# Part of a recurrence moved beside another stage's product, and attention tiles in alternating order

## The chip, the cores and the metric

One core of a Trainium2 chip runs the whole program once. The metric is the device time of one execution in microseconds, taken as the median of several runs. A profile of one further execution shows every instruction of TensorE (PE), its weight loads (PEld), VectorE (DVE), ScalarE (ACT), GpSimd (POOL) and the DMA queues.

## What is computed

Two blocks follow one another on 1024 tokens of width 1024, in fp32. The change touches the second block, after its input projection:

```python
q, k, v, xr, gr = jnp.split(proj, [...], axis=-1)       # 4 heads x 2 x 64 of q and k, 512 v, 512 xr, 512 gr
q = partial_rope(rms_norm_2(q, q_norm_w[l]), cos, sin)
k = partial_rope(rms_norm_2(k, k_norm_w[l]), cos, sin)
lam = exp(sum(lambda_q1 * lambda_k1)) - exp(sum(lambda_q2 * lambda_k2)) + lambda_init
attn = diff_attention(q, k, v, lam)                     # (softmax_0 - lam * softmax_1) @ v, causal, tiles of 128 queries
attn = rms_norm_2(attn, subln_w[l]) * (1.0 - lambda_init)
xc = causal_dwconv(xr, conv_rnn_w[l], conv_rnn_b[l])    # 4 taps
y = rg_lru(xc, w_gate_a[l], b_gate_a[l], w_gate_x[l], b_gate_x[l], lru_lambda[l])
y = rms_norm_2(y * jax.nn.gelu(gr), rnn_norm_w[l])
x = x + jnp.concatenate([attn, y], axis=-1) @ w_out[l]
```

In rg_lru two gates r and i are sigmoids of block-diagonal products of xc; a = exp(-8 r softplus(-lambda)), u = sqrt(1 - a^2) i xc, and h[t] = a[t] h[t-1] + u[t] along the 1024 tokens.

## The kernel before

Stages follow one another, each a block in which every engine has its own in-order list of instructions and waits on semaphores. The order of work is written out by hand. Names and lines are those of the program in the profile.

**mix** (line 2195) merges the first block's branches, projects them with w_out, normalizes, and multiplies by the second block's input weights. Products of fp32 accuracy are made of three matmuls on split operands (product3). After 128 tiles of merging come j = 0 to 31, tiles of 128 channels x 512 tokens: 16 for q and k, 8 for xr, 8 for gr. VectorE evicts each one with a per-token factor (L2555); turn_head (L2481 to L2488) normalizes and rotates q and k; ScalarE makes the head norms with Ln and Exp and then gelu of gr (L2361). Then come j = 32 to 47, the v product: 16 tiles of 128 tokens x 256 channels in two column halves c, evicted by ScalarE (L2368). Six PSUM buffers rotate; two more banks (6 and 7) are for sums.

**attend** (line 2582) makes attention and the recurrence together. Its 32 units n are (head h, query tile t), t from 0 to 7, of width (t+1)*128 keys. For unit n:
- TensorE: sc(n), the scores of both softmaxes into one set of four PSUM banks (L2656), with the mask added (L2659); then tr(n-1), the transposes (L2667); then av(n-2), the product with v (L2678). sc(n) waits for both exponentials of n-1.
- VectorE: soft(n-1), the combination of the two softmaxes (L2883 to L2890), then peak(n, 0) and peak(n, 1), the maxima (L2876).
- ScalarE: exp(n, 0) and exp(n, 1) with their sums (L2738), turn_out(n-1), the copy of the transposes (L2746), take(n-2), the copy of the output (L2753).

The setup of small vectors stands before unit 0 (L2845 to L2867). After a head: square, mean, norm, scale, flip (L2699) and end (L2771, L2772). One channel group of the recurrence goes with each head: tap (convolution, L2914, L2917), gates (L2693, 128 x 128 weights, two halves of 512 tokens), open_a, open_x, decay, decay2, bend, rise on ScalarE (L2778 to L2806), and admit, spare, enter, run, leave on VectorE (L2922 to L2943; run is the scan over tokens, L2937). Each is hung on a fixed tile t of the head. The stage ends with the last head's end; then **out_up** (line 2980) begins, with the output projection.

The ring of two weight buffers feeds each product in split form: ring.load on SyncE waits until the buffer's low part is cut (ring.cut), split_hi on ScalarE (L138) and split_lo on VectorE (L145) make the two parts.

## Time and profile before

| | us |
|---|---|
| median of 3 runs | 4651.68 (4647.18 to 4652.19) |
| the profiled execution's own time | 4653.29 |
| its span | 4651.5 |
| TensorE busy | 4501.1 (97%) |
| VectorE busy | 2670.2 (57%) |
| ScalarE busy | 1727.7 (37%) |
| mean granted clock of TensorE | 0.985 |

A page has busy time by engine, the span in slices, queues, a chain and groups of instructions. The stage of attention lies between 3547.7 and 3748.7 us of the span, the v product of mix just before it. A timeline shows instructions in order of their start, with equal neighbours merged, and in brackets how long the engine had stood idle and what released it. The granted clock is 1.00 at 2.4 GHz and 0.50 at 1.2 GHz.

### The profile page before, as it was taken

To read this page: it belongs to the slowest core of one execution; us is meant where nothing else is said; L and a number is where in the kernel's file an instruction comes from. 1 tells how busy PE (TensorE), PEld (TensorE's weight loads), DVE (VectorE), ACT (ScalarE), POOL (GpSimd) and SP (SyncE) were. 2 spreads that over 40 slices of the span, in tenths; PEclk is the share of its full clock that TensorE was granted. 3 is DMA by queue.
4 is the path that set the end of the run, shared out by engine and by line. 5 is a ranking of instruction groups with operands and counts; after the bars stand their busy time and mean duration, and the time that the engine had idled before them with its cause. 6 is when DMAs were issued, how large, how long until landed. Compare 5 with 4: busy or idle time off the path is not lost. (4 is left out here: it accounts for less than half of the span.)

```text
span 4651.5 us, 66517 instructions
## 1 busy us (share of the span) xinstructions
PE 4501.1 (97%) x27608; PEld 3667.2 (79%) x27608; DVE 2670.2 (57%) x3938; ACT 1727.7 (37%) x2924; POOL 457.6 (10%) x371
## 2 busy tenths in 40 slices
PE   7999999999999999999999799899998789999999
PEld 4888877778999999999999444688776567888887
DVE  3245545555637777777777676546453755555543
ACT  3234443444424544455444333211343742111111
POOL 0000000000002333332336000000010000000000
PEclk9999999999999999999999999999999899999999
DMA  5244344434430110111021352433210021122222
GB/s 210 99 144 151 130 147 141 145 131 150 168 120 15 46 57 30 64 41 59 28 102 45 98 178 86 155 108 109 82 46 19 19 113 63 70 77 73 100 87 95
DMA packets 155978, 441.79 MB, mean 95 GB/s; under 512 B 17168, under 2 KB 47120, under 8 KB 140448
## 3 DMA queue, kind: packets, MB, share of 16 engines
q1 hardware_dynamic: 140624, 383.98, 23.5%
q0 software_dynamic: 9296, 32.58, 2.0%
q10 hardware_dynamic: 5760, 20.97, 1.2%
q8 instruction: 221, 3.62, 0.3%
q14 instruction: 77, 0.63, 0.0%
HBM read 294.86 MB, written 141.56 MB: 94 GB/s over the span
## 5 line engine op out<-in xcount | busy, mean ns | idle before, releaser
L202 PE MATMUL pr_ps<-uhl,w_split 128*128 128x512 f32 (+1 forms) x1520 | 586.7, 386 | 3.1 <-DVE w_split L145 2.2
L206 PE MATMUL pr_ps<-uhl,w_split 128*128 128x512 f32 (+1 forms) x1520 | 571.9, 376 | 0.0
L205 PE MATMUL pr_ps<-uhl,w_split 128*128 128x512 f32 (+1 forms) x1520 | 571.2, 376 | 0.0
L1583 DVE TENSOR_TENSOR b_G<-b_ps,cst 128x512 fp32r<-128x512 f32 x560 | 381.5, 686 | 65.0 <-PE b_ps L1362 61.7
L138 ACT ACTIVATE w_split<-share 128x2048 fp32r<-128x2048 f32 x64 | 122.6, 1915 | 701.1 <-DVE ou_vc L3305 271.1
L202 PEld LDWEIGHTS pr_ps<-uhl,w_split 128*128 128x128 f32 x1520 | 287.0, 189 | 81.4 <-issue 29.2
L205 PEld LDWEIGHTS pr_ps<-uhl,w_split 128*128 128x128 f32 x1520 | 287.1, 189 | 56.0 <-issue 5.8
L206 PEld LDWEIGHTS pr_ps<-uhl,w_split 128*128 128x128 f32 x1520 | 286.8, 189 | 52.3
L1124 POOL TENSOR_SCALAR b_Mr<-b_tri 128x512 fp32r<-128x512 f32 x80 | 117.8, 1489 | 1878.9 <-DVE b_tri L1567 1878.9
L202 PE MATMUL ou_ps<-ou_a,w_split 128*128 128x512 f32 x704 | 277.5, 394 | 7.7 <-DVE ou_a L2160 7.7
L205 PE MATMUL ou_ps<-ou_a,w_split 128*128 128x512 f32 x704 | 275.6, 391 | 0.0
L206 PE MATMUL ou_ps<-ou_a,w_split 128*128 128x512 f32 x704 | 275.3, 391 | 0.0
L776 DVE COPY pr_stage<-pr_ps 128x256 f32<-128x256 f32 (+1 forms) x92 | 49.7, 540 | 391.7 <-PE pr_ps L206 391.6
L202 PE MATMUL mx_ps<-mx_a,w_split 128*128 128x512 f32 x640 | 258.1, 403 | 13.4 <-DVE mx_a L2160 13.4
L1214 ACT ACTIVATE b_EY<-b_ps 128x512 fp32r<-128x512 f32 x320 | 192.4, 601 | 183.1 <-PE b_ps L1376 183.1
L206 PE MATMUL mx_ps<-mx_a,w_split 128*128 128x512 f32 x640 | 255.3, 399 | 0.0
L205 PE MATMUL mx_ps<-mx_a,w_split 128*128 128x512 f32 x640 | 254.0, 397 | 0.0
L1362 PE MATMUL b_ps<-b_G,b_EY 128*128 128x128 f32 x1600 | 244.8, 275 | 0.0
L1362 PEld LDWEIGHTS b_ps<-b_G,b_EY 128*128 128x128 f32 x1600 | 222.4, 190 | 12.6 <-issue 12.0
L206 PE MATMUL ou_ps<-ou_ext,w_split 128*128 128x512 f32 x576 | 224.4, 390 | 0.0
L202 PE MATMUL ou_ps<-ou_ext,w_split 128*128 128x512 f32 x576 | 224.3, 389 | 0.0
L205 PE MATMUL ou_ps<-ou_ext,w_split 128*128 128x512 f32 x576 | 224.3, 389 | 0.0
(498 smaller groups left out, 10045.5 us busy)
## 6 DMA issues: line engine op xcount, KB each, us to landing
w_ring<-in_w_in SPq DMA_DIRECT2D x41, 1024.0 KB, 5.3
proj<-pr_stage SPq DMA_DIRECT2D x160, 256.0 KB, 2.0
share<-in_w_up SPq DMA_DIRECT2D x24, 1024.0 KB, 4.8
ar<-share SPq DMA_DIRECT2D x32, 512.0 KB, 2.8
b_AR<-ar SPq DMA_DIRECT2D x64, 256.0 KB, 2.9
pr_raw<-proj SPq DMA_DIRECT2D x48, 256.5 KB, 3.4
ada<-in_ada_w SPq DMA_DIRECT2D x24, 512.0 KB, 5.8
ff<-ou_vc ACTq DMA_DIRECT2D x24, 512.0 KB, 2.6
```

The source lines that it names most:

```text
L138: self.nc.scalar.activation(self.hl[:, n % NBUF, 0], raw, ACT.Copy).then_inc(self.hi_done, 1)
L202: mm = nc.tensor.matmul(dst, a[0], b[0], start=start, stop=False)
L205: nc.tensor.matmul(dst, a[0], b[1], start=False, stop=False)
L206: return nc.tensor.matmul(dst, a[1], b[0], start=False, stop=stop)
L776: V.tensor_copy(dst, src).then_inc(taken[1], 1)
L1124: F[x]["pool"].done(ts(Mr[x][:], tri[x][e][:], 1.0, None, ALU.mult), f"{n}.Mr")
L1214: L[x]["act"].done(A(EY[x][:, 0:2], both(x)[:, 0:2], ACT.Copy), f"{n}.low{m}")
L1362: mm = mmul(bank(x, 0)[:, q * P:(q + 1) * P], E[x][:, q] if m else Mr[x][:, q], Gs[x][m % 2][:, q], start=True, stop=True)
L1583: L[x]["dve"].done(V.tensor_tensor(Gs[x][m % 2][:], heads(x, 0 if m else 1), rep(K(f"lev{m}"), 4), ALU.mult), f"{n}.G{m}")
```

## The change

In mix, the small vectors of the recurrence and lambda are made between the evictions of the q/k product (lower at j = 4, rates at j = 20). The convolutions of all four channel groups run on VectorE from j = 28 on; the gates, the ScalarE passes and the scans of groups 0 and 1 run beside the v product, and their results are written over gr. Gates use PSUM banks 6 and 7. Buffers are taken from the weight ring's raw halves, from xr of the two done groups and from the rope table. In attend, groups 2 and 3 are left, their convolutions (in the former table) already there; their steps are hung on chosen units from n = 1 to 9 and 12 to 25. Odd heads take their tiles from 7 down to 0. The norm of a head's output is done in five groups (three whole heads, then two halves of head 3), one half of each head's last copy goes to VectorE, and the sums of exponentials are kept, so that a copy per unit goes. Table sets of ScalarE are loaded at written places. TensorE gets small products of ones after units 17 and 18 and before the last flip. Cut to the lines that the text speaks of (scale, mean, square, norm and end take a group g instead of a head; they and the recurrence's steps are otherwise as before):

```diff
+        few = small(rn)
+        lp, lam, sub_w, hb, l0, l1 = (few[n] for n in ("lp", "lam", "sub_w", "hb", "l0", "l1"))
+        early_w, late_w = ([ring.buf[:, (ring.base + 2 * RP + l) % NBUF].rearrange("p k c -> p (k c)")[:, f * T:(f + 1) * T] for f in range(2)] for l in (8, 9))
+        xc = [table[:, 0], table[:, 1]]
+        wg = early_w[1].rearrange("p (a k c) -> p a k c", a=2, k=RT)
...
                     ring.load(sp, w2[n] if n < 8 else w_v2[n - 8], 0, 0, 2 * RP + n, split=True)
+                sp.wait_ge(ring.cut, ring.split_base + 2 * RP + 11)
+                sp.dma_start(wg[:, 0], w_ga).then_inc(wg_in, 16)
...
+                nc.scalar.preload_act_table_set("natural_log_exp_and_others")
...
+                nc.scalar.preload_act_table_set("exp_and_others")
...
+                def rise(k):
+                    nc.scalar.preload_act_table_set("sqrt_and_others")
+                    act.wait_ge(m_ready, k + 1)
+                    A(tt[k], tt[k], ACT.Sqrt, scale=0.25).then_inc(rt, 1)
+                    nc.scalar.preload_act_table_set("exp_and_others")
...
+                    if j == 33:
+                        open_a(0)
+                    if j == 35:
+                        open_x(0)
+                        bend(0)
+                        decay(0)
+                        decay2(0)
+                    if j == 37:
+                        open_a(1)
+                        rise(0)
+                    if j == 39:
+                        open_x(1)
+                        bend(1)
+                    if j == 40:
+                        decay(1)
+                        decay2(1)
+                    if j == 41:
+                        rise(1)
                 act.wait_ge(bent, 8)
...
+                def gates(k, x):
+                    if x:
+                        pe.wait_ge(th_a, k + 1)
+                    else:
+                        pe.wait_ge(conv, k + 1)
+                        if k:
+                            pe.wait_ge(th_x, k)
+                        else:
+                            pe.wait_ge(wg_in, 32)
+                            pe.wait_ge(h_log, KT)
+                    for half in range(2):
+                        mm = nc.tensor.matmul(ps[:, 6 + half], wg[:, x, k], xc[k][:, half * HALF:(half + 1) * HALF], start=True, stop=True)
+                    mm.then_inc(gate_x if x else gate_a, 1)
                 for c in range(2):
...
+                        if c == 0 and t % 2 == 0:
+                            gates(t // 4, t // 2 % 2)
...
+                    if j >= 28:
+                        tap(0, j - 28)
                 ring.split_lo(dve, 2 * RP + 9)
+                for j in range(4):
+                    tap(1, j)
+                for k in range(2):
+                    admit(k)
+                    spare(k)
+                    enter(k)
+                    run(k)
+                    leave(k)
+                    for j in range(4):
+                        tap(k + 2, j)
                 dve.wait_ge(h_done, KT)
                 dve.wait_ge(taken, N1 + 32)
+                dve.wait_ge(conv, RT)
...
+    NR = 2
...
-        units = [(h, t) for h in range(A_HEADS) for t in range(T // P)]
+        units = [(h, 7 - t if h % 2 else t) for h in range(A_HEADS) for t in range(T // P)]
...
+        groups = [(0, 0, 8), (1, 0, 8), (2, 0, 8), (3, 4, 8), (3, 0, 4)]
+        rows_done = [8, 16, 24, 28, 32]
...
                 for k in range(RT):
-                    sp.wait_ge(y_ready, k + 1)
-                    sp.dma_start(cat[:, 4 + k], y[:, k % 2]).then_inc(y_stored[k % 2], 16)
-                for b in range(2):
-                    sp.wait_ge(y_stored[b], 8 * RT)
+                    if k >= RT - NR:
+                        sp.wait_ge(y_ready, k - (RT - NR) + 1)
+                    sp.dma_start(cat[:, 4 + k], gr[:, k]).then_inc(y_stored, 16)
+                sp.wait_ge(y_stored, 16 * RT)
...
+                def keep_warm(times):
+                    for _ in range(times):
+                        nc.tensor.matmul(ps[:, 1, 0:P], G["ones"][:], G["ones"][:], start=True, stop=True)
                 for n in range(NU):
-                    h, t = units[n]
                     sc(n)
-                    if t == 1:
-                        gates(h, 0)
-                    if t == 2:
-                        gates(h, 1)
-                    if t == 0 and h >= 2:
-                        pe.wait_ge(exp_ready, 2 * n)
-                        flip(h - 2)
+                    if n in (1, 12):
+                        gates(n // 12, 0)
+                    if n in (2, 13):
+                        gates(n // 12, 1)
+                    if n == 15:
+                        flip(0)
+                    if n == 28:
+                        flip(1)
+                    if n == 30:
+                        flip(2)
                     if n >= 1:
                         tr(n - 1)
                     if n >= 2:
                         av(n - 2)
+                    if n == 17:
+                        pe.wait_ge(head_out, 2)
+                    if n in (17, 18):
+                        keep_warm(4)
                 tr(NU - 1)
                 av(NU - 2)
-                pe.wait_ge(exp_ready, 2 * NU)
-                flip(A_HEADS - 2)
+                flip(3)
                 av(NU - 1)
-                flip(A_HEADS - 1)
+                pe.wait_ge(head_out, 6)
+                keep_warm(8)
+                flip(4)
 
...
+                    if n in (3, 14):
+                        bend(n // 12)
+                    if n in (4, 20):
+                        decay2(n // 20)
+                    if n in (5, 21):
+                        decay(n // 20)
+                    if n in (6, 22):
+                        nc.scalar.preload_act_table_set("sqrt_and_others")
+                        rise(n // 20)
+                        nc.scalar.preload_act_table_set("natural_log_exp_and_others")
+                    if n == 9:
+                        square(0)
+                    if n == 11:
+                        norm(0)
+                        nc.scalar.preload_act_table_set("exp_and_others")
+                    if n == 15:
+                        end(0, 0)
+                    if n == 17:
+                        square(1)
+                    if n == 23:
+                        norm(1)
+                    if n == 25:
+                        square(2)
+                    if n == 27:
+                        norm(2)
+                    if n == 28:
+                        end(1, 0)
+                    if n == 29:
+                        square(3)
+                    if n == 30:
+                        end(2, 0)
                 turn_out(NU - 1)
                 take(NU - 2)
+                norm(3)
                 take(NU - 1)
-                square(A_HEADS - 1)
-                end(A_HEADS - 2)
-                norm(A_HEADS - 1)
-                end(A_HEADS - 1)
+                square(4)
+                end(3, 1)
+                norm(4)
+                end(4, 0)
...
+                    if n in (3, 14):
+                        admit(n // 12)
+                    if n in (5, 21):
+                        spare(n // 20)
+                    if n in (7, 23):
+                        enter(n // 20)
+                    if n in (8, 24):
+                        run(n // 20)
+                    if n in (9, 25):
+                        leave(n // 20)
+                    if n == 10:
+                        mean(0)
+                    if n == 12:
+                        scale(0)
+                    if n == 15:
+                        end(0, 1)
+                    if n == 18:
+                        mean(1)
+                    if n == 26:
+                        scale(1)
+                    if n == 27:
+                        mean(2)
+                    if n == 28:
+                        end(1, 1)
+                    if n == 29:
+                        scale(2)
+                    if n == 30:
+                        mean(3)
+                        end(2, 1)
                 soft(NU - 1)
-                leave(RT - 1)
-                mean(A_HEADS - 1)
-                scale(A_HEADS - 1)
-                dve.wait_ge(y_ready, RT)
+                scale(3)
+                mean(4)
+                scale(4)
+                dve.wait_ge(y_ready, NR)
 
 
 FT = 24
@@ -3393,13 +3588,13 @@
```

## Rows read from the trace of the kernel before

**Rows 1.** The page's first line.
```profile
span 4651.5 us, 66517 instructions
```
**Rows 2.** Windows, one for each head: busy us (and instructions) by engine, granted clock, DMA.
```profile
core 0: us, PE busy (x) PEld busy (x) DVE busy (x) ACT busy (x) POOL busy (x), PEclk, DMA share, GB/s
...
3548.00:3592.00 44.00, 29.42 (x144) 17.20 (x144) 33.16 (x69) 29.29 (x60) 0.00 (x0) 0.84 0.11 36
3592.00:3637.00 45.00, 34.80 (x180) 24.27 (x180) 34.68 (x63) 31.70 (x65) 0.00 (x0) 0.85 0.03 13
3637.00:3684.00 47.00, 35.88 (x190) 24.68 (x190) 34.61 (x63) 32.89 (x66) 0.56 (x1) 0.85 0.06 23
3684.00:3730.00 46.00, 37.27 (x188) 26.03 (x188) 31.59 (x60) 32.73 (x66) 0.54 (x1) 0.81 0.06 24
```
**Rows 3.** Timeline, one widest tile: start, us, engine, line, operation, [idle before].
```profile
3631.11 1.99 PE L2656 MATMUL at_ps<-qk 64*128 64x512 f32 x8 [1.60 <-ACT at_p L2738]
...
3633.39 2.35 DVE L2876 TENSOR_REDUCE at_nb<-at_ps 128x1 f32<-128x1024 f32 x2
...
3634.65 1.11 ACT L2738 ACTIVATE at_p<-at_ps,at_nb 128x1024 f32<-128x1024 f32 x1 [2.73 <-DVE at_nb L2876]
...
3637.03 0.49 PE L2656 MATMUL at_ps<-qk 64*128 64x128 f32 x4 [1.29 <-ACT at_p L2738]
```
**Rows 4.** Timeline of TensorE, head 0: scores of tiles 0, 1, 5 and 6.
```profile
3548.33 0.49 PE L2656 MATMUL at_ps<-qk 64*128 64x128 f32 x4
...
3554.05 1.22 PE L2656 MATMUL at_ps<-qk 64*128 64x256 f32 x4 [4.86 <-ACT at_p L2738]
...
3573.09 1.56 PE L2656 MATMUL at_ps<-qk 64*128 64x512 f32 x8 [1.50 <-ACT at_p L2738]
...
3577.93 1.77 PE L2656 MATMUL at_ps<-qk 64*128 64x512 f32 x8 [1.11 <-ACT at_p L2738]
```
**Rows 5.** Timeline of TensorE, after the first tile of head 2.
```profile
3640.89 1.97 PE L2667 MATMUL at_ps<-cst,at_p 128*128 128x128 f32 x8 [2.09 <-DVE at_p L2890]
...
3645.77 0.83 PE L2656 MATMUL at_ps<-qk 64*128 64x256 f32 x4
```
**Rows 6.** Timeline of TensorE: a gate product and what follows it.
```profile
3602.12 1.93 PE L2693 MATMUL at_ps<-at_xc,at_wg 128*128 128x512 f32 x4
3603.89 0.27 PE L2667 MATMUL at_ps<-cst,at_p 128*128 128x128 f32 x1
```
**Rows 7.** Windows, the v product from its second tile on (columns as in rows 2).
```profile
3503.60:3546.80 43.20, 43.16 (x360) 42.95 (x358) 2.29 (x1) 8.92 (x17) 0.00 (x0) 1.00 0.00 1
```
**Rows 8.** Timeline of ScalarE: a table load and the activation after it.
```profile
3620.52 1.28 ACT L2765 ACT_TABLE_LOAD   x1
3621.82 0.21 ACT L2765 ACTIVATE at_fac<-at_fac 128x8 f32<-128x8 f32 x1
```
**Rows 9.** Groups by line, attention: busy us, mean ns | idle before.
```profile
L2917 DVE SCALAR_TENSOR_TENSOR at_xc<-xg,par,at_xc 128x1024 f32<-128x1024 f32 x12 | 15.3, 1275 | 0.1
...
L2937 DVE TENSOR_TENSOR_SCAN at_xc<-at_aa,at_ix 128x1024 f32<-128x1024 f32 x4 | 9.1, 2280 | 0.0
...
L2797 ACT ACTIVATE at_a<-at_ra,at_hb 128x1024 f32<-128x1024 f32 x4 | 5.1, 1287 | 0.0
...
L2922 DVE SCALAR_TENSOR_TENSOR at_ix<-at_ix,at_xc 128x1024 f32<-128x1024 f32 x4 | 4.9, 1216 | 0.0
```
**Rows 10.** Timeline, from the last exponential to the next stage.
```profile
3729.85 0.19 ACT L2738 ACTIVATION_READ_ACCUMULATOR at_p<-at_ps,at_nb 128x1 f32 x1
...
3738.11 0.28 ACT L2753 ACTIVATE at_raw<-at_ps 128x128 f32<-128x128 f32 x1 [2.38 <-PE at_ps L2678]
...
3741.48 1.28 ACT L2765 ACT_TABLE_LOAD   x1
...
3748.74 0.63 ACT L166 ACTIVATE w_split<-share 128x512 fp32r<-128x512 f32 x1 [0.97 <-PEq L2586]
```
**Rows 11.** Windows, the start of the next stage (columns as in rows 2).
```profile
3748.70:3756.00 7.30, 4.37 (x12) 3.47 (x13) 6.34 (x8) 6.06 (x8) 0.00 (x0) 0.55 0.91 359
```

More of the change, by code:

```diff
@@ L2489, in _, with run, leave @@
+                def run(k):
+                    dve.wait_ge(u_ready, 2 * k + 2)
+                    dve.wait_ge(ex, k + 1)
+                    V.tensor_tensor_scan(xc[k], aa[k], ix[k], 0.0, ALU.mult, ALU.add).then_inc(scan, 1)
+                def leave(k):
+                    dve.wait_ge(scan, k + 1)
+                    dve.wait_ge(bent, 8)
+                    V.tensor_tensor(gr[:, k], xc[k], gr[:, k], ALU.mult).then_inc(left, 1)
                 for k in range(HK):
@@ L2641, in _ @@
             def _(pe):
-                pe.wait_ge(lstep, 1)
-                nc.tensor.matmul(ps[:, 7, 0:2], K("heads64"), lp[:], start=True, stop=True).then_inc(lam_s, 1)
                 pe.wait_ge(rounded, 2)
@@ new lines, in end, with open_a @@
+                def end(g, x):
+                    h = groups[g][0]
+                    act.wait_ge(flipped, g + 1)
+                    if h >= 2:
+                        act.wait_ge(head_stored[h % 2], 16)
+                    A(out[:, h % 2, x * HALF:(x + 1) * HALF], flat_at(h, x), ACT.Copy, scale=sub_w).then_inc(head_out, 1)
+                def open_a(q):
+                    k = RT - NR + q
+                    act.wait_ge(gate_a, q + 1)
+                    if q:
+                        act.wait_ge(tn, q)
```

422 lines of the change are left out of this document (224 added, 198 removed).

## The prediction

> **What bounds the kernel now.** Read the page first: TensorE is busy nearly everywhere, and only one stretch of the 4651.5 us span stands out [rows 1]. The table of windows by head of attention shows it [rows 2]: from 3548 to 3730 TensorE is busy 29 to 37 us of each 44 to 47, at a mean granted clock of 0.81 to 0.85. No engine is full there; VectorE and ScalarE have 32 to 35 and 29 to 33. So the time of a head is a chain of hand-overs, and the next view is the timeline of one tile. A widest tile (1024 keys) runs from the start of its scores at 3631.11 to the start of the next tile's scores at 3637.03, 5.92 us: 2.28 for the scores and the mask, 1.26 to the first exponential, then two exponentials [rows 3]. There is one score buffer, so the next scores wait for the second exponential. That is the floor of a tile. The 768-key tile needs 4.84 us in the same way [rows 4]. Taking a straight line through the two, 0.54 per 128 keys, 128 keys need 2.14, and the eight tiles of a head 8 x (5.92 + 2.14) / 2 = 32.2 us. The heads take 44 to 47 us [rows 2]. All four spend 3730.04 - 3548.33 = 181.7 us [rows 4, 10], against a floor of 129: 53 us of excess.
>
> Where the excess sits: at a change of head a 128-key tile follows a 1024-key one. Its scores start at 3637.03, and the next tile's only at 3645.77, 8.7 us instead of 2.1, because TensorE waits until 3640.89 for VectorE's late difference and then transposes and multiplies the wide tile [rows 3, 5]. VectorE is late because the scan (2.28 us) and a tap (1.28 us) are queued ahead of it [rows 9]. Three such changes cost 6.6 each, 20 us. The start costs about 3.7 more than a tile's floor (second scores at 3554.05, the first at 3548.33, floor 2.1) [rows 4]. The rest, some 29 us, is spread: gates on TensorE, table loads on ScalarE, VectorE's recurrence, half clock.
>
> The merge's v product is the opposite case: TensorE 43.16 of 43.20 us at clock 1.00, VectorE 2.29, ScalarE 8.92 [rows 7]. It has room on both helpers and none on TensorE.
>
> **The change part by part.**
>
> *Work put into the v window, TensorE.* Four gate products (two channel groups). In attention one occupies TensorE from 3602.12 to the next product at 3603.89, 1.77 us [rows 6]. 4 x 1.77 = 7.1 us, all on the path since nothing is idle there. The extra two-column sum beside the token factors is a few tenths at most; I take 0.
>
> *The same, ScalarE and VectorE.* Do their waits stop TensorE? I laid the orders out with a v tile of 2.88 us (43.2 us / 15 tiles, rows 7) and about 1.3 us per full pass, 2.28 for the scan [rows 9]. gates(0,0) needs the first convolution, whose four taps sit one each behind the last four evictions, done before the first v tile is. gates(0,1) comes two v tiles (5.8 us) after gates(0,0) and needs two half-width tanh passes behind one copy: done about 1 us early. gates(1,0) needs the x tanh of group 0, also about 1 us early. gates(1,1) needs open_a(1), also about 1 us early. ScalarE's copies of v fall up to some 5 us behind, under the six buffers (17 us) that TensorE may run ahead. VectorE must do 16 taps (4 before the window, 12 in it, 15 us), two scans and eight passes (14 us), with waits for two square roots between table loads; I find its last tap 4 to 5 us before the lengthened product ends. So 0 for waits, with up to 5 as the upper bound. The gate weights' transfers are queued on SyncE behind the last weight loads; SyncE has nothing else to do there. The v copies queued behind ScalarE's waits are the only work held.
>
> *Setup and table loads.* The small vectors (lower, rates) go to VectorE between evictions of the q/k product, where TensorE sets the pace; 0. In attention, nineteen loads (counted in the groups by line) become about five. The timeline shows what a load costs: it starts at 3620.52 and the next activation at 3621.82, 1.30 us [rows 8]. Fourteen fewer are 18 us of ScalarE, of which the path sees what isn't under scores and reduction. The Trainium skill ("ScalarE: Activation LUTs", What ACT_TABLE_LOAD costs) gives about 2.66 us for a switch, a drain counted in; by that it would be 37 us of ScalarE. The row shows no such drain in front or behind, so the sum goes by 1.30.
>
> *Attention's floor and what is left on it.* The tiles are the same, so 129 us stays. Running odd heads from wide to narrow puts 1024 beside 1024 and 128 beside 128, so the three changes of 6.6 go. Does TensorE then bind in the falling heads, where small scores stand before big transposes? Head 1 has 34.8 us busy at 0.85 [rows 2], about 29.6 at full rate, less two gate products (3.5) 26, against the floor of 32.2: no, at full clock. What I put back, tile by tile: the four gate products left (1.77 each, part under slack) 4.1; two square roots between two loads, 3.6 us each, against the 3.5 or less that ScalarE has free between tiles, 1.1 each, 2.2; means and scales of a head on VectorE (1.2 us passes) 3.3; three flips of eight transposes at narrow tiles 1.4; bend, norm and a table preload 1.4; two scans 0.7. Sum 13 us. Bounds: 5, if the slack takes most, and 25, about what such work costs now (the 29 of the spread excess, less half the recurrence).
>
> *Clock.* The clock falls to its half level in short spells in all heads (means 0.81 to 0.85 [rows 2]). It costs the path between 0 and 12 us now: 1.5 us each time a wide score meets it. With fewer waits TensorE is busier, roughly 26 of 36 us per head at full rate instead of 30 of 45. I take 6. The filler products of ones in keep_warm stand where TensorE waits anyway.
>
> *The tail.* Now 3730.04 (end of the last exponential) to 3748.74, 18.7 us [rows 10]. The last tile is the widest, so the steps to its copy-out end at 3738.1 (8.1 us), and the head's norm handles eight blocks, with a table load. After the change the last tile is the narrowest and only four blocks are left: I estimate 2.5 for the tile's steps; 2.4 for group 3's scale and flip, queued in front of the last product on TensorE; and for the last group half-width versions of square, mean, scale, flip and copy with small hand-overs, 6.4. Together 11.3, bounds 9 and 14. If group 3's chain weren't in front, 9.
>
> *Next stage.* It starts at a clock of 0.55 [rows 11]. Its first products might gain up to 1.8 us if the fillers held the clock, but TensorE still stands idle after the last flip. I take 0.
>
> Sum for attention: 129 + 13 + 6 + 11.3 = 159.3, against 200.4 now (3548.33 to 3748.74 [rows 4, 10]): -41.1. The longer start is inside that figure. With +7.1 for the v window, -34.0. On the span, 4651.5 - 34.0 = 4617.5. The profiled execution took 4653.29 us, 1.6 more than the median of the runs shown, 4651.68, so the median should be 4617.7; I say **4618**.
>
> A cross-check by another road: VectorE loses 16 taps (12 of 1.28 us and 4 shorter ones, 18.5 us), half the recurrence's passes and scans (about 14) and 32 small copies (5) and gains about 3, 34 us out of attention, where it queues in front of the path most often.
>
> **The rivals.**
> 1. *Only the named holes close.* The spread excess stays because other hand-overs take the place of those removed. Then the gain is 20 (changes of head) + 3.7 (start) + 7.4 (tail) - 7.1 = 24: **4628**. For it: moved means, scales and flips sit at narrow tiles that have least slack. Against: 14 loads and half the recurrence do leave. Chance 0.17.
> 2. *The recurrence outlasts the v product.* A late th_x or the tap behind the group's scan holds gates on TensorE or the stage's end. Each late microsecond beyond the 4 to 5 of slack counts fully; at 5 us: **4623**. For it: three gates have only about 1 us to spare. Chance 0.08.
> 3. *The table preloads don't do what they say*: loads are still placed before each Ln or Exp. At most 14 x 1.30, some 8 of it on the path: **4626**. Chance 0.03.
> 4. *Slower than before: half clock through the falling heads.* TensorE's 26 us of a head are 52 at half rate, against a floor of 32: +20 a head. One head so: **4638**. From two upward the gain is gone, and all four give 4618 + 80 - 6 = **4692**. For it: every head has spells now, and narrow tiles leave TensorE idle between short bursts. Against: the clock came back within each head so far, and the mean stays over 0.8 [rows 2]. The Trainium skill ("TensorE: Matmul & The Clock Gate", Part 1) says that how busy the array has recently been sets the clock, which speaks for more clock, not less. Chance 0.03 for slower, 0.03 for one head.
>
> **How the numbers follow.** Forecast 0.66, with 4608 to 4627 as its own range (extras 5 to 20, clock 0 to 12, tail 9 to 14, not all at one end). Rivals 1 to 3 lie between 4620 and 4632. The range reaches to **4606 to 4635**. A change of 0.2% (9 us) is about what a measurement of this kernel can tell from none. Faster by more: all cases but the last, **0.95**; within: **0.02**, a rival met by another; slower: **0.03**.
>
> **What would show it.** Right: the v stretch about 7 us longer with TensorE still at 1.00 and no idle in front of the gate products; 5.9 us for the tiles on both sides of the first change of head and about 2 at the second; five or six table loads in attention; a tail of about 11 us; attention about 159 us. Wrong: TensorE idle before a gate product or at the merge's end; falling tiles above the floor with the clock at 0.5; VectorE's mean or scale in front of a score reduction by more than a microsecond.

## The result, and the profile after

The changed kernel takes 4604.79 us (median of 4, 4603.9 to 4609.25) against 4651.93 (4647.18 to 4653.58): a ratio of 0.99, 95% interval 0.9888 to 0.9913. That is 47 us, where 34 were forecast and 45.7 was the far end of the range; the median lies 1.2 us below 4606, the range's end. The same program timed once more gave 4607.02 (run 9). The profiled execution's span is 4603.0 us against 4651.5 [rows 1]; all stage times below are from profiled executions.

The path, cut at the first and the last copy of v (their starts), attention's first scores, the end of the last exponential and the first split of the next stage:

| stretch | before | after | difference | forecast |
|---|---|---|---|---|
| start to first copy of v | 3503.68 | 3502.53 | -1.15 | 0 |
| first to last copy of v | 43.11 | 49.55 | +6.44 | +7.1 |
| last copy to first scores | 1.54 | 1.43 | -0.11 | 0 |
| first scores to last exponential | 181.71 | 137.73 | -43.98 | -33.7 |
| tail | 18.70 | 10.27 | -8.43 | -7.4 |
| next stages | 902.76 | 901.49 | -1.27 | 0 |

Windows of the kernel after: the v product, the four heads, the tail, and the start of the next stage (busy us and instructions by engine, granted clock, DMA), to be held against [rows 2, 7, 10, 11].

```profile
core 0: us, PE busy (x) PEld busy (x) DVE busy (x) ACT busy (x) POOL busy (x), PEclk, DMA share, GB/s
3502.50:3553.51 51.01, 49.55 (x377) 45.57 (x375) 30.76 (x25) 27.96 (x37) 0.00 (x0) 1.00 0.00 1
3553.51:3588.78 35.27, 25.98 (x142) 15.76 (x142) 22.58 (x41) 25.48 (x54) 0.00 (x0) 0.95 0.22 68
3588.78:3624.86 36.08, 33.22 (x220) 24.10 (x220) 29.45 (x51) 25.95 (x58) 0.00 (x0) 1.00 0.04 16
3624.86:3657.53 32.67, 23.64 (x158) 16.56 (x157) 23.53 (x47) 24.25 (x56) 0.56 (x1) 1.00 0.04 17
3657.53:3691.24 33.71, 30.51 (x219) 23.47 (x219) 30.90 (x56) 23.13 (x57) 0.54 (x1) 1.00 0.08 32
3691.24:3701.51 10.27, 4.22 (x33) 3.49 (x31) 3.54 (x11) 4.06 (x12) 0.00 (x0) 0.93 0.00 0
3701.51:3708.80 7.29, 4.40 (x10) 3.47 (x11) 6.37 (x8) 6.07 (x8) 0.00 (x0) 0.50 0.91 357
```

The heads fell from 44 to 47 us to 33 to 36, and the clock from which they are run rose: 0.95 and three times 1.00, where it was 0.81 to 0.85. VectorE's work in attention fell from 140.4 to 110.0 us. The v product has TensorE busy 49.55 of 51.01 us at 1.00.

Single rows of TensorE: a gate product in head 0, the scores on both sides of the first change of head (1024 keys twice), a gate product in head 1, and the first scores behind the second change (128 keys).

```profile
3556.39 3.47 PE L2868 MATMUL at_ps<-cst,at_wg 128*128 128x512 f32 x4
...
3588.78 1.99 PE L2839 MATMUL at_ps<-qk 64*128 64x512 f32 x8 [2.37 <-ACT at_p L2925]
...
3594.72 1.45 PE L2839 MATMUL at_ps<-qk 64*128 64x512 f32 x6 [1.11 <-ACT at_p L2925]
...
3610.94 1.93 PE L2868 MATMUL at_ps<-cst,at_wg 128*128 128x512 f32 x4
...
3624.86 0.49 PE L2839 MATMUL at_ps<-qk 64*128 64x128 f32 x4
```

From 3588.78 to 3594.72 it is 5.94 us, the floor of a widest tile, where [rows 5] had 8.7. (The row at 3594.72 is cut short where the view ends; the scores there take 1.77 us.) The gate product at 3556.39 takes 3.47 us instead of 1.93: that is the half level, the only spell of it that tells in the four heads' periods. The tail, on ScalarE:

```profile
3691.04 0.20 ACT L2925 ACTIVATION_READ_ACCUMULATOR at_p<-at_ps,at_nb 128x1 f32 x1
...
3693.12 0.29 ACT L2954 ACTIVATE at_fac<-at_ms,eps 128x4 f32<-128x4 f32 x1
...
3699.91 0.69 ACT L2963 ACTIVATE share<-at_ps,rn 128x512 f32<-128x512 f32 x1 [1.67 <-PE at_ps L2879]
3701.51 0.63 ACT L166 ACTIVATE w_split<-share 128x512 fp32r<-128x512 f32 x1 [0.92 <-PEq L2770]
```

No table load is left in it. The kernel before has two, at 3731.04 and at 3741.48 [rows 10]; behind the first ScalarE stands idle for 1.35 us, so only the second is on the path.

### The profile page after: what moved, and what is told of

It reads as the page before. It is cut to its first block and busy times, and to the rows that moved or that the text cites. A ratio compares the mean times of both kernels' runs of the same rounds, so it can differ in the third digit from the quotient of the medians.

```text
span 4603.0 us, 66523 instructions
## 1 busy us (share of the span) xinstructions
PE 4479.9 (97%) x27640; PEld 3653.9 (79%) x27640; DVE 2672.4 (58%) x3919; ACT 1685.9 (37%) x2891; POOL 458.2 (10%) x371
```

## The experiments

All are compared with the kernel before run on the same chip, 4652 to 4654 us. Of each, D is the time from the first scores to the end of the last exponential, in the one execution that was profiled; before has 181.71, after 137.73. A tile's period is the time from the start of its scores to the start of the next tile's. A spell is a short time in which TensorE's clock is at its half level.

**1. Table loads.** after, with the written loads taken out of attention:

```diff
-                        nc.scalar.preload_act_table_set("sqrt_and_others")
                         rise(n // 20)
-                        nc.scalar.preload_act_table_set("natural_log_exp_and_others")
...
                         norm(0)
-                        nc.scalar.preload_act_table_set("exp_and_others")
```

> The changed kernel with the table sets of attention left to the compiler again (those of the merge stay written). Loads return in front of each Ln and each Exp after it, 1.30 us each. Theory P (path): the norms of heads 1 and 2 cost about 1.6 us each after ScalarE's slack, the two in the tail 1 and 2.6 us each, 6 to 9 us in all. Rival: the slack between tiles takes those inside the heads, and only the tail pays, about 3 us. If the clock depends on gaps, a spell or two at the half level may come with them.

Measured: 4611.89 us (4610.52 to 4615.39), ratio 0.9913 (0.9898 to 0.9928), 7 us more than after. There are 14 loads in attention instead of 5. D is 140.75 (+3.0) and the tail 16.05 (+5.8). ScalarE in the tail:

```profile
3703.78 1.28 ACT L2954 ACT_TABLE_LOAD   x1
3705.07 0.30 ACT L2954 ACTIVATE at_fac<-at_ms,eps 128x4 f32<-128x4 f32 x1
3705.39 1.28 ACT L2956 ACT_TABLE_LOAD   x1
```

Each norm needs two loads, one for its logarithm and one for its exponential, because without the written set the two don't share one. Nine loads of 1.28 us are 11.5 us of ScalarE; the path paid 8.8 of them, and two thirds of that in the tail, where nothing runs beside them. The activation starts 0.01 us behind the load, so a load costs its 1.28 and no more. Theory P (6 to 9 us) holds, with more of it in the tail than it gave: 5.8 instead of 3.6.

**2. The order of the tiles.** after, with all heads from narrow to wide, and the steps hung on the units where their inputs are then ready:

```diff
-        units = [(h, 7 - t if h % 2 else t) for h in range(A_HEADS) for t in range(T // P)]
-        groups = [(0, 0, 8), (1, 0, 8), (2, 0, 8), (3, 4, 8), (3, 0, 4)]
+        units = [(h, t) for h in range(A_HEADS) for t in range(T // P)]
+        groups = [(0, 0, 8), (1, 0, 8), (2, 0, 8), (3, 0, 4), (3, 4, 8)]
```

> The changed kernel with all heads from narrow to wide, its hooks for gates, norms and flips moved to narrow tiles accordingly and the last group being tiles 4 to 7. Theory W (width): a 128-key tile behind a 1024-key one costs some 6 us more than its floor by itself, because TensorE must transpose and multiply the wide tile first; three changes give 18 us, the wide last tile 5 to 7 us: +23 to +27 us in all, and more with half-level spells at the changes. Theory Q (queue): it was the scan and the taps in front of the difference on VectorE that made the changes dear, and they are gone or moved; then a change costs 2 us or less over the floor and the total rises by 9 to 13 us.

Measured: 4625.88 us (4621.67 to 4629.84), ratio 0.9944 (0.9928 to 0.9961), 21 us more than after. D is 148.24 (+10.5), the tail 19.20 (+8.9). TensorE at the second change of head:

```profile
3622.68 0.49 PE L2842 MATMUL at_ps<-qk 64*128 64x128 f32 x4 [1.45 <-ACT at_p L2928]
...
3624.45 1.67 PE L2853 MATMUL at_ps<-cst,at_p 128*128 128x128 f32 x8 [0.91 <-DVE at_p L3080]
3625.91 2.83 PE L2862 MATMUL at_ps<-share,at_aT 128*128 128x128 f32 x14
3628.68 0.70 PE L2842 MATMUL at_ps<-qk 64*128 64x256 f32 x4
```

6.00 us from the 128-key scores to the next, instead of 8.74. TensorE waits 0.91 us for the difference, not 2.09 [rows 5], because no scan stands in front of it. The transposes and the product take 1.67 and 2.83 us, where run 6 has 1.09 and 1.73 at the full level: about 1.7 of the 6.00 us are the clock, which fell again with the old order. So the alternating order is worth 19.4 us, nearly half of it in the tail, and a part of that is clock. Neither theory came out. The three changes take 6.66, 6.00 and 5.95 us, 4.0 to 4.7 over the floor of 1.97 us, which lies between Q's 2 and W's 6, and so does the total.

**3. Half the recurrence out of attention, alone.** before, without the taps, gates, passes and scans of groups 2 and 3; they are left out altogether:

```diff
+    RK = 2
-                    if t == 1:
+                    if t == 1 and h < RK:
                         gates(h, 0)
```

> The kernel before, with the recurrence of channel groups 2 and 3 left out of attention (their taps, gates, ScalarE passes and scans; only the last multiplication stays), so that heads 0 and 1 carry a recurrence and heads 2 and 3 carry none. By the prediction's cross-check VectorE's work sets the pace, and each head without it is 8 to 9 us shorter: -16 to -18 us. If the chain of hand-overs hides it, heads 2 and 3 shrink by 3 us each or less. Theory G expects the half-level spells at the changes of head to stay, since the gap behind the wide tile stays; fewer elsewhere.

Measured: 4636.56 us (4631.26 to 4638.1), ratio 0.9963 (0.9948 to 0.9977), 17 us less than before. D is 164.50 (-17.2). Windows of heads 2 and 3, and the scores of the first two tiles of head 3:

```profile
3639.64:3677.24 37.60, 27.79 (x180) 19.63 (x180) 25.93 (x56) 23.57 (x56) 0.56 (x1) 0.95 0.07 29
3677.24:3713.24 36.00, 27.79 (x180) 20.10 (x180) 25.10 (x54) 23.52 (x56) 0.54 (x1) 0.95 0.07 30
...
3677.24 0.49 PE L2660 MATMUL at_ps<-qk 64*128 64x128 f32 x4 [1.44 <-ACT at_p L2742]
...
3680.01 1.73 PE L2682 MATMUL at_ps<-share,at_aT 128*128 128x128 f32 x14
3681.67 0.70 PE L2660 MATMUL at_ps<-qk 64*128 64x256 f32 x4
```

Heads 2 and 3 fall by 9.3 and 10.1 us, and their clock rises to 0.95, so a part of the fall is clock. Heads 0 and 1, whose work is as before, take 1.4 and 0.8 us more, and the tail 0.8 more. With the old order and full clock (the product takes 1.73 us) a change of head takes 3681.67 - 3677.24 = 4.43 us.

**4. What is left of the recurrence in after.** Here too the work of groups 2 and 3 is left out:

```diff
-                    if n in (1, 12):
-                        gates(n // 12, 0)
-                    if n in (2, 13):
-                        gates(n // 12, 1)
```

(and the passes and scans behind them)

> The kernel after, with the recurrence of channel groups 2 and 3 left out of attention (gates, ScalarE's passes, the scans; the last multiply by the gelu stays), so its output is not the recurrence's. One step of the forecast priced what is left of the recurrence at about 9 us for the two groups (gates 4.1, square roots 2.2, bend and scans 2). The two heads that carry it took 71.35 us in the kernel after, the two that carry little of it 66.38. Theory P (what is left is paid only where it meets the path): the first two heads fall to 65 to 66.5 us, the third and fourth by about 1, the kernel by 6 to 8 us. Rival K (it costs what it costs in the kernel before, where leaving two groups out took 18 us off heads 2 and 3): 15 us or more.

Measured: 4602.3 us (4600.98 to 4603.66), ratio 0.9896 (0.9881 to 0.991), 2.5 us less than after. D is 132.55 (-5.2). The four heads:

```profile
3555.24:3590.02 34.78, 25.91 (x135) 16.91 (x135) 19.35 (x38) 17.24 (x45) 0.00 (x0) 0.80 0.23 68
3590.02:3622.72 32.70, 29.87 (x212) 22.66 (x212) 26.35 (x49) 22.47 (x53) 0.00 (x0) 1.00 0.05 18
3622.72:3654.47 31.75, 23.65 (x159) 16.58 (x158) 21.34 (x45) 19.66 (x51) 0.56 (x1) 1.00 0.04 17
3654.47:3687.79 33.32, 30.30 (x219) 23.41 (x219) 28.90 (x55) 23.10 (x57) 0.54 (x1) 1.00 0.08 33
```

Head 1 fell by 3.4 us, heads 2 and 3 by 0.9 and 0.4. Head 0 fell by only 0.5, since its clock is 0.80: three tiles (384 to 640 keys) have periods 0.9 to 1.3 us over the undisturbed ones, 3.3 us in all. So the expectation for the first two heads (65 to 66.5) was missed, at 67.48, and so was the one for the kernel (6 to 8 us less). Set aside those 3.3 and the 1.7 of after's own spell, and what is left of the recurrence costs 5.2 + 3.3 - 1.7 = 6.8 us, where the forecast had 9; in the kernel before, two groups cost 17 to 19. Rival K, 15 us or more, falls. The two figures don't price the same work, since run 3 takes out the taps too, which after has moved. The clock of head 0 fell from 0.95 to 0.80; whether that is because of the work taken out isn't shown.

**5. VectorE's queue.** before, without taps 1 to 3 of each group, so the convolution is incomplete:

```diff
-                    if t >= 4 and h + 1 < RT:
-                        tap(h + 1, t - 4)
+                    if t == 4 and h + 1 < RT:
+                        tap(h + 1, 0)
```

> The kernel before with taps 1 to 3 of each channel group left out of attention (tap 0 stays), so the convolution is not complete. It takes 12 passes of 1.28 us, 15.3 us, from VectorE and nothing else. Theory Q (VectorE's queue in front of the late difference and of the score reductions is what a head pays): the changes of head fall from 8.74 to about 7.5 us, the tiles that a tap follows from 6.29 and 6.53 to 5 to 5.5, 12 to 16 us in all. Rival S (the taps lie under slack, and the price of the recurrence is in the gates and ScalarE's passes): less than 5 us.

Measured: 4645.71 us (10 runs, 4640.2 to 4650.0), ratio 0.9987 (0.9977 to 0.9996), 6.5 less than before; the profiled execution lies 12 below that of before, and its D is 170.61 (-11.1), its tail 20.30 (+1.6). TensorE at a change of head:

```profile
3628.97 0.49 PE L2656 MATMUL at_ps<-qk 64*128 64x128 f32 x4 [1.44 <-ACT at_p L2738]
...
3631.62 1.97 PE L2667 MATMUL at_ps<-cst,at_p 128*128 128x128 f32 x8 [0.89 <-DVE at_p L2890]
3633.38 2.48 PE L2678 MATMUL at_ps<-share,at_aT 128*128 128x128 f32 x14
...
3635.79 0.70 PE L2656 MATMUL at_ps<-qk 64*128 64x256 f32 x4
```

The change takes 6.82 us, 1.9 less than before: the wait for the difference is 1.2 us shorter, about one tap, and the product is 0.7 us shorter because the clock is back within it (2.48 us against 3.20). So a tap does stand in front of the late difference. The three changes give 5.8 us together and the second tile of head 0 gives 2.0. The 896-key tiles, which the expectation saw shorter by 1 us or more, are unchanged at 6.53. The other 3.3 us of the 11.1 are spells at other places: the 768-key tiles of heads 1 and 3, for instance, fall from 6.29 to the 5.55 that head 2 of the kernel before has with its taps. So the 15.3 us of taps are paid at the changes of head and at the start, for less than 7.8 us; elsewhere they lie under slack, as rival S had it. That fits the median's 6.5 better than D does.

**6. The clock in the kernel before.** before, with products of ones where TensorE stands idle, and nothing else:

```diff
+                    if t == 0 and h:
+                        pe.wait_ge(aT_ready, n - 1)
+                        keep_warm(4, 6)
...
+                    if t in (3, 5, 6, 7):
+                        pe.wait_ge(taken, n - 2)
+                        keep_warm(6 + (n - 1) % 2, 4)
```

> The kernel before with products of ones on TensorE where it stands idle in attention: six between the scores and the transposes at each change of head, four behind the output product of tiles 3, 5, 6 and 7. Everything else stays. Theory C (the half-level spells follow from idle stretches, and cost the path where they meet wide tiles): the mean granted clock of the heads rises from 0.81 to 0.85 to over 0.95, the scores of the widest tile take 1.99 instead of 3.47 us and the product behind the change of head 1.95 instead of 3.2, and the kernel gets 8 to 13 us shorter. Rival N (spells do not cost the path, as a term of 0 would have it, or the fillers take what they give): within 3 us. The forecast's term was 6.

Measured: 4644.17 us (10 runs, 4638.32 to 4647.48), ratio 0.9984 (0.9975 to 0.9994), 8 less than before. D is 168.06, 13.65 us less; the tail is 21.58, 2.9 more, at a clock of 0.70, where before has 0.81. The four heads and the tail, then the transposes and output product at a change of head, and the scores of a widest tile:

```profile
3548.71:3590.76 42.05, 31.29 (x175) 20.29 (x174) 32.90 (x66) 29.02 (x60) 0.00 (x0) 0.88 0.11 38
3590.76:3632.28 41.52, 34.24 (x224) 24.82 (x225) 34.64 (x63) 31.57 (x64) 0.00 (x0) 1.00 0.04 14
3632.28:3674.55 42.27, 35.11 (x232) 25.68 (x232) 34.63 (x63) 32.64 (x66) 0.56 (x1) 1.00 0.06 26
3674.55:3716.77 42.22, 34.72 (x232) 25.57 (x232) 31.95 (x60) 32.59 (x66) 0.54 (x1) 1.00 0.07 26
3716.77:3738.35 21.58, 10.18 (x54) 9.59 (x54) 6.66 (x11) 9.30 (x15) 0.00 (x0) 0.70 0.06 25
...
3636.13 1.09 PE L2667 MATMUL at_ps<-cst,at_p 128*128 128x128 f32 x8 [0.75 <-DVE at_p L2899]
3637.06 1.73 PE L2678 MATMUL at_ps<-share,at_aT 128*128 128x128 f32 x14
...
3668.63 1.99 PE L2656 MATMUL at_ps<-qk 64*128 64x512 f32 x8 [1.31 <-ACT at_p L2747]
```

The same instructions in the kernel before, at the half level:

```profile
3642.64 3.20 PE L2678 MATMUL at_ps<-share,at_aT 128*128 128x128 f32 x14
...
3676.42 3.47 PE L2656 MATMUL at_ps<-qk 64*128 64x512 f32 x8 [2.18 <-ACT at_p L2738]
```

1.73 instead of 3.20 us, 1.99 instead of 3.47. Theory C holds: all work is still there, TensorE does more, and the four heads are 13.65 us shorter; 6.9 of that are the three changes of head (8.74 to 6.44 us each). With the idle stretches filled the spells go, and they had cost the heads that much in the profiled executions. The tail, which got no fillers, gave 2.9 us of it back, which leaves 10.8. The median shows 8.0, with an interval of 2.8 to 11.6.

**7. The fillers in after.** after without them:

```diff
-                    if n in (17, 18):
-                        keep_warm(4)
...
-                pe.wait_ge(head_out, 6)
-                keep_warm(8)
```

> The changed kernel without the products of ones (after units 17 and 18, and before the last flip). Theory G (gaps): TensorE's clock now stays full in attention because its long gaps are gone; the fillers add little. Then attention up to its last exponential stays at 137 to 139 us and the total moves by 0 to +2 us, all in the tail, where the last flip may run at the half level. Theory F (fillers): they hold the clock. Then half-level spells come back, several a head, and the total rises by 5 us or more.

Measured: 4609.82 us (4607.6 to 4612.92), ratio 0.9908 (0.9893 to 0.9922). D is 139.96 (+2.2), the tail 11.40 (+1.1). Head 2 and the tail:

```profile
3629.83:3664.74 34.91, 25.80 (x142) 17.38 (x141) 23.64 (x47) 24.25 (x56) 0.56 (x1) 0.85 0.04 16
3698.45:3709.85 11.40, 3.55 (x17) 2.56 (x15) 3.54 (x11) 4.05 (x13) 0.00 (x0) 0.64 0.00 0
```

Head 2's clock falls from 1.00 to 0.85 and it takes 34.91 instead of 32.67 us; the other heads are within 0.02 of after. The tail's clock falls from 0.93 to 0.64. So 3.4 us are the fillers', 2.2 of them in head 2, which took 32.67 to 32.69 us in all five profiles of the changed order that keep the fillers and head 2's work. Each theory is right in part: three of the four heads keep their clock without fillers, head 2 and the tail don't. The rest of the 5 us lies ahead of attention, where the code is the same (run 9).

**8. The v window.** Two kernels: after with narrow gate products (so the gates are wrong), and after with seven more multiplies on VectorE behind the last tap.

```diff
-                        mm = nc.tensor.matmul(ps[:, 6 + half], wg[:, x, k], xc[k][:, half * HALF:(half + 1) * HALF], start=True, stop=True)
+                        mm = nc.tensor.matmul(ps[:, 6 + half, 0:32], wg[:, x, k], xc[k][:, half * HALF:half * HALF + 32], start=True, stop=True)
```

> The kernel after with the four gate products beside the v product cut to 32 of 512 columns (the rest of what the tanh reads is stale, so the recurrence of groups 0 and 1 is wrong). All waits stay. Theory O (the 6.4 us that the v stretch grew are TensorE's occupancy by the gates): first to last copy of v falls from 49.55 to 43 to 44 us, and then VectorE's last tap, 3.6 us ahead of the last copy now, or close to it, decides when attention starts: 4 to 6 us off the kernel. Rival W (the growth is waits of TensorE for ScalarE or VectorE): the stretch stays above 46 us and the kernel gains less than 3.

Measured: 4601.75 us (4599.68 to 4605.9), ratio 0.9895 (0.9878 to 0.9911). First to last copy of v takes 44.49 us, 5.06 less, and the first scores still start 1.42 behind it. So 5.1 of the 6.4 us are the gates' columns, and at most 1.4 (44.49 against 43.11) is all else, of which the narrowed products themselves are a part. Theory O holds for the cause; the stretch came out 0.5 us over the 43 to 44 that it gave. The last tap ends at 3546.47, 2.25 us before the last copy starts, so VectorE doesn't decide even then. Attention has D 138.73, since the first gate product met a longer spell, and the tail is 0.7 us longer, so the kernel gained 3.0 us and not 4 to 6.

```diff
+                for i in range(7):
+                    dve.wait_ge(conv, RT + i)
+                    V.tensor_tensor(tt[1], xc[0], xc[1], ALU.mult).then_inc(conv, 1)
```

> The kernel after with seven more full-width multiplies (about 1.24 us each, 8.7 us) on VectorE behind the last tap beside the v product; their result is not used. The forecast gave VectorE 4 to 5 us of room there; the trace of after has its last tap end 3.6 us before the last copy of v starts. If VectorE's lateness counts fully past its room, attention's first scores start 8.7 - 4 = 4.5 to 5 us later behind the last copy of v than the 1.4 us of after; if something else hides it, less than 2.

Measured: 4612.58 us (4610.35 to 4615.45), ratio 0.9914 (0.9899 to 0.9929). VectorE, the last taps, the extra work and the stage's first cast; and then, of after, the last taps and the last copy of v:

```profile
3543.71 3.93 DVE L2630 SCALAR_TENSOR_TENSOR cst<-xg,par,cst 128x1024 f32<-128x1024 f32 x3
3547.68 8.78 DVE L2755 TENSOR_TENSOR share<-cst 128x1024 f32<-128x1024 f32 x7
3556.98 0.23 DVE L3063 CAST at_id_r<-cst 128x128 fp32r<-128x128 f32 x1 [0.53 <-PEq L2258]
```

```profile
3544.60 3.92 DVE L2630 SCALAR_TENSOR_TENSOR cst<-xg,par,cst 128x1024 f32<-128x1024 f32 x3
...
3552.08 0.47 ACT L2434 ACTIVATE share<-mx_ps,mx_tk 128x256 f32<-128x256 f32 x1 [2.37 <-PE mx_ps L206]
```

The first scores come 6.22 us behind the last copy, 4.8 more than in after, where 4.5 to 5 were expected. Of 8.78 us of lateness 4.0 were free: from the end of the taps in after, 3548.52, to the end of the last copy, 3552.55.

**9. after again, and two variants.** after unchanged; v3_both, with the second pair of gates on units 17 and 18 in place of the fillers and twelve products of ones at the start of the next stage; v4_start, with eight more at the start of attention.

```diff
-                    if n in (1, 12):
-                        gates(n // 12, 0)
+                    if n in (1, 17):
+                        gates(n // 17, 0)
...
+                for _ in range(12):
+                    nc.tensor.matmul(ps[:, 7, 0:P], G["ones"][:], G["ones"][:], start=True, stop=True)
```

> The kernel after, unchanged, beside its variants. The stretches that no edit touched have differed by several us between programs with the same code there (the first copy of v at 3498 to 3507 us). If that is the program's layout, a second profile of the same program puts the first copy of v at 3502.5, attention's first scores at 3553.5 and the next stage at 3701.5, each within 0.5; if it is chance of the execution, they move by 2 to 5 us again, while the lengths of the undisturbed tiles stay to 0.02 us.

Measured: 4607.02 us (4603.72 to 4609.62). The first copy of v is at 3501.67, 0.86 earlier than in the first profile; D is 137.70 against 137.73, the tail 10.28 against 10.27, and the same gate product takes 3.44 us at the half level. Attention repeats to 0.03 us; the stretch before it moved by more than the 0.5 us of a fixed layout and by less than the 2 to 5 us of chance, so which of the two it is stays open. Among programs with the same code there, each profiled once, the first copy of v lies between 3498.39 (run 2) and 3507.51 (run 7), and much of such differences is there early. One and the same transfer, some 105 us into the span, is issued at 103.10 us in run 2 and at 108.55 in run 7 (granted clock of the first 100 us 0.93 and 0.88), and at 105.76 and 104.87 in the two profiles of after.

> The kernel after with two edits. (1) The gates of channel group 3 leave units 12 and 13, where tiles fall and TensorE has no slack (periods 1.43 and 1.97 us over the undisturbed ones), for units 17 and 18, where tiles rise and TensorE stood idle 1.2 to 1.3 us, in place of the fillers there. (2) Twelve products of ones on TensorE at the start of the next stage, where it stands idle 2.9 us before its first product. Theory: units 12 and 13 shorten by 2.5 to 3, units 17 to 19 lengthen by 1 to 2, and the first products of the next stage take 0.23 instead of 0.43 us, 2.5 us; together 3 to 5 us less than after. Rival: ScalarE's and VectorE's passes, which move along, cost the rising tiles what TensorE gains, and the fillers come too early to hold the clock: within 1.5 us of after.

Measured: 4605.07 us (4604.46 to 4610.03), no different from after, where 3 to 5 us less were expected. Units 12 and 13 are 3.0 us shorter, 17 and 18 1.4 longer, as expected. D is 135.11, 2.6 less than after, but 1.6 of that is the second tile of head 0, which ran without its spell, and 0.8 went to a new spell at the first tile of head 1. The next stage's start:

```profile
3701.68 5.46 PE L3349 MATMUL ou_ps<-ones 128*128 128x128 f32 x24 [1.66 <-PEq L2770]
3706.79 0.62 PE L202 MATMUL ou_ps<-ou_a,w_split 128*128 128x512 f32 x1
3707.25 0.39 PE L205 MATMUL ou_ps<-ou_a,w_split 128*128 128x512 f32 x1
```

The fillers run at the half level for 5.1 us and put off the first product by 2.24 us; the products behind them then come every 0.23 us. What the clock gave, the delay took: the next stages take 901.44 us against 901.49.

> v3_both with eight more products of ones: five before attention's first scores and three behind them, where TensorE stands idle 1.5 and 1.1 us, ahead of the half-level spell in which the first gate product took 3.47 instead of 1.93 us. If the idle start brings that spell, it goes and the first head gets 1.6 us shorter than in v3_both; if not, within 0.5 of it.

Measured: 4606.96 us (4603.12 to 4610.3). The first gate product, and the scores of the first two tiles of head 1:

```profile
3555.39 1.93 PE L2872 MATMUL at_ps<-cst,at_wg 128*128 128x512 f32 x4
...
3586.14 3.45 PE L2841 MATMUL at_ps<-qk 64*128 64x512 f32 x8 [2.37 <-ACT at_p L2927]
...
3593.68 1.77 PE L2841 MATMUL at_ps<-qk 64*128 64x512 f32 x8 [1.07 <-ACT at_p L2927]
```

The gate product takes 1.93 us, but it did so in v3_both too, so the start's fillers aren't shown to have done it. They put the first scores off by 0.9 us (2.29 behind the last copy of v instead of 1.42). Two spells now meet widest tiles (3586.14, 3.45 us; the first of head 3 likewise takes 7.63 instead of 5.94 us), and D is 137.57. No version beats after by more than can be measured.

## Why the prediction was wrong, point by point

The mechanisms were right and the sum was 14.5 us short on the span: 34 forecast, 48.5 found. Of that 11.3 are in attention: 159.3 forecast, 137.73 + 10.27 = 148.0 found. The forecast time, 4618, is 13.2 us over the median. That the median lies just outside the stated range rather than just inside is within what executions differ by: the repetition's 4607.02 is inside. The size of the miss isn't. By its terms:

- **Clock, 6 forecast, about 1.7 found.** This is the largest miss, -4.3. The step that failed is "It costs the path between 0 and 12 us now ... I take 6". Half of the upper bound was left in the sum without a row that says how much stays. In the heads of the kernel before it cost 13.65 (run 6, 10.8 with the tail), and after keeps one spell of it, 4.52 us for the second tile of head 0 instead of the 2.88 of v3_both. The bound was a little low too: it was made from wide scores alone (1.5 each), and the transposes and the output product at a change of head (1.97 and 3.20 us instead of 1.09 and 1.73) weren't counted. They stood inside the 6.6 of each change. What was said of the direction, that a busier TensorE has fewer spells, held.
- **Extras, 13 forecast, 10.0 found, -3.0.** Found are the periods of after less the undisturbed ones, 11.7, less the clock's 1.7. The gates of head 1 cost 1.4 and 2.0, those of head 0 0.3 and 0.9; square roots 0 and 0; multiplies at units 7 and 23 (enter) 0.9 each. The square roots between two loads, 2.2 in the forecast, were hidden. The other 3.6 lie on eight tiles, at most 0.7 each, and aren't taken apart here. All of the recurrence in attention cost 6.8, not 9 (run 4).
- **Floor, 129 forecast, 126.0 found, -3.0.** The undisturbed tiles are 1.97, 2.53, 3.09, 3.65, 4.22, 4.77, 5.34 and 5.94 us, 31.5 a head and not 32.2. The straight line went through [rows 4]'s 4.84, a tile that is 0.07 over its floor, and so put 128 keys at 2.14.
- **Tail, 11.3 forecast, 10.3 found, -1.0.** Group 3's scale and flip were in front of the last product, as said. Taken out of after one at a time, the order is worth 8.9 in the tail (run 2) and the loads 5.8 (run 1). Together that is more than the 8.4 that the tail lost, so how they divide it isn't shown.
- **v window, +7.1 forecast, +6.4 found.** No wait stopped TensorE, and VectorE had 4.0 us of room where 4 to 5 were given (run 8). Rival 2 didn't come about, and its rule, that lateness past the room counts fully, was right.
- **Setup and next stage, 0 forecast, -2.5 found.** The first part lies within what the same code shows from one profiled execution to another (9.1 us, run 9); the next stages, whose code is the same, took 901.3 to 903.1 us over the profiles of the changed kernel's variants. So nothing is made of them, though without them the time would have been in the range. The next stage started at a clock of 0.50, 0.55 before, and gained nothing by it, as forecast.

"So the three changes of 6.6 go" was right in sum and wrong in its reason. A change took 8.74 us; at full clock 6.44 (run 6), at full clock without the recurrence in VectorE's queue 4.43 (run 3), in the alternating order 1.97 or 5.94, the floor. So of 6.8 us over the floor, 2.3 are clock, 2.0 the recurrence's work, and 2.5 the order. Rival 1, that other hand-overs take the place of those removed, is refuted: the periods of after are 11.7 us over the floor in all, where the spread excess alone was some 29. Rival 3 didn't come about, with 5 loads in attention; by run 1 the loads are worth 8.8 us, close to the "some 8" that it gave. Rival 4, half clock through the falling heads, didn't happen: they ran at 1.00. The Trainium skill ("TensorE: Matmul & The Clock Gate", Part 1) had spoken for more clock, not less, and the trace agrees: TensorE is busy for 82% of D instead of 75%, and its mean clock is 0.99 instead of 0.84. Of the about 2.66 us that the Trainium skill gives for a table switch with its drain ("ScalarE: Activation LUTs", What ACT_TABLE_LOAD costs), the rows again show 1.28 to 1.30.

Where the gain comes from, by taking single parts away: order 19.4 (run 2), half the recurrence 16.4 (run 3, D and tail), table sets 8.8 (run 1), fillers 3.4 (run 7). The four add up to 48.0, and attention lost 52.4 us. But they were measured around two different kernels and overlap in the clock, so the sum is no proof and the remaining 4.4 aren't assigned.

## What to carry to other kernels

In a stage that runs below clock 1.00, look up each slow instruction's full-rate duration, price the difference everywhere it stands on the path, and say which of these the change removes, instead of taking a middle value. Work queued on a helper in front of a hand-over is paid two ways, once by its wait and once by the clock that TensorE loses while it waits; moved to where the helper is idle and TensorE full, the gates cost only their 1.6 us a product and the helper's work nothing. Take the floor of a tile from several undisturbed tiles, and not from a line through two. And before the price of a part is read from a sum over tiles, as in run 5, take out the tiles where a spell came or went: here each moved 0.7 to 1.7 us.

## What the runs showed of the hardware

- Half-level spells change place from program to program, even where the code of the stage is the same up to there: the gate product of unit 1 meets one in after and in its repetition (3.47, 3.44 us), and takes 1.93 in v3_both, whose attention is that of after before unit 12, and in v4_start. In v4_start spells meet two widest tiles (7.54 and 7.63 us instead of 5.94). With an unchanged program attention repeated to 0.03 us.
- Products of ones started from a half-level clock run at the half level themselves: 24 records took 5.46 us, where 16 took 1.95 in the tail. The products behind them then came every 0.23 instead of 0.43 us, but 2.24 us later.
- A table load is 1.28 us in all loads looked at, with the activation 0.01 to 0.02 us behind it where that waits for nothing else.
- Executions of one program differ by some 6 us (4603.7 to 4609.6), and 5.5 of the 9.1 us between two programs with the same code ahead of attention were there within the first 109 us, with the clock at 0.88 in the later and 0.93 in the earlier one.
